# Value projections of two attentions moved behind the attentions' first scores

## The reference

```python
# first block, per layer (4 heads of 64 columns)
logits = q @ k.T * scale + f_q[:, None] - f_k[None, :]      # f: running sum of log forget gates
probs  = softmax(where(key_pos <= q_pos, logits, -inf))
out    = probs @ v                                          # v = h @ w_in[:, value columns]
# second block: for each of 3 groups of 4 heads (windows of 128, 512, 2048; dilations 1, 4, 16)
s = q_block @ k_block.T * scale + band_mask
p = softmax(s);  o = p @ v_block;  lse = log(sum(exp(s)))
out = sum over groups of softmax(lse over groups) * o
```

## Time and profile before

| | us |
|---|---|
| time, median of 3 runs (4006.53 to 4017.21) | 4011.14 |
| time of the profiled execution | 4007.0 |
| span in its trace | 4005.2 |
| PE busy | 3704.3 (92%) |
| DVE busy | 1721.3 (43%) |
| ACT busy | 1155.8 (29%) |
| POOL busy | 712.6 (18%) |

### The profile page before, as it was taken

One profiled execution on the slowest core, in us unless ns is written; L12 is line 12 of the kernel. 1 busy time (PEld: TensorE's weight loads), 2 busy tenths in 40 slices (PEclk: granted clock), 3 DMA queues, 4 the chain that ended last, 5 costly groups with the idle time before them and its releaser, 6 DMA issues. The chain is left out here.

```text
span 4005.2 us, 67440 instructions
## 1 busy us (share of the span) xinstructions
PE 3704.3 (92%) x29462; PEld 2800.3 (70%) x29462; DVE 1721.3 (43%) x3002; ACT 1155.8 (29%) x2208; POOL 712.6 (18%) x248
## 2 busy tenths in 40 slices
PE   6899998998999989899879999998899999999998
PEld 5564666886646668778757777776687568787876
DVE  6644545456445454621674544544003253223233
ACT  1427233114272331301544444443101121001011
POOL 2110003221100032122021111110221012322321
PEclk9999899999999999999989999999899999999999
DMA  4131201221302012312110000000222211111112
GB/s 155 40 95 38 66 12 61 78 74 43 95 19 84 12 57 81 126 34 72 61 36 19 25 25 28 26 24 23 72 63 86 91 42 43 53 42 53 42 49 109
DMA packets 190182, 225.67 MB, mean 56 GB/s; under 512 B 20991, under 2 KB 168001, under 8 KB 187081
## 3 DMA queue, kind: packets, MB, share of 16 engines
q1 hardware_dynamic: 189896, 221.47, 16.8%
HBM read 188.89 MB, written 32.56 MB: 55 GB/s over the span
## 5 line engine op out<-in xcount | busy, mean ns | idle before, releaser
L193 POOL CAST weights_high<-weights_value 128x2048 fp32r<-128x2048 f32 x34 | 67.0, 1970 | 1289.3 <-DMA weights_value<-in_w_in_dram 691.5
L208 PE MATMUL banks<-h_high,weights_high 128*128 128x512 f32 x608 | 241.2, 397 | 8.1 <-PEq L820 5.1
L208 PE MATMUL banks<-h_high,weights_low 128*128 128x512 f32 x608 | 238.9, 393 | 0.0
L208 PE MATMUL banks<-ffn_in_high,ffn_weights_high 128*128 128x512 f32 x512 | 203.9, 398 | 8.4 <-PEq L75 8.1
L208 PE MATMUL banks<-ffn_in_low,ffn_weights_high 128*128 128x512 f32 x512 | 203.6, 398 | 0.0
L208 PE MATMUL banks<-ffn_in_high,ffn_weights_low 128*128 128x512 f32 x512 | 203.4, 397 | 0.0
L208 PE MATMUL banks<-ffn_weights_high,hidden_high 128*128 128x512 f32 x512 | 199.2, 389 | 0.0
L208 PE MATMUL banks<-ffn_weights_low,hidden_high 128*128 128x512 f32 x512 | 199.2, 389 | 0.0
L208 PE MATMUL banks<-ffn_weights_high,hidden_low 128*128 128x512 f32 x512 | 199.2, 389 | 0.0
L4244 ACT ACTIVATE hidden_value<-banks 128x512 f32<-128x512 f32 x64 | 38.3, 598 | 555.7 <-PE banks L208 555.6
L208 PE MATMUL banks<-h_high_again,pair_weights_high 128*128 128x512 f32 x384 | 180.3, 469 | 7.1 <-PEq L2293 7.1
(11 more groups left out here) (479 smaller groups left out, 9153.5 us busy)
## 6 DMA issues: line engine op xcount, KB each, us to landing
ffn_weights_value<-in_w_ff_dram SPq DMA_DIRECT2D x32, 1024.0 KB, 5.4
weights_value<-in_w_in_dram SPq DMA_DIRECT2D x24, 1024.0 KB, 5.2
attention_scratch<-in_ada_w_dram SPq DMA_DIRECT2D x12, 1024.0 KB, 5.3
pair_weights_value<-in_w_in_dram SPq DMA_DIRECT2D x24, 512.0 KB, 4.0
ndow_weights_value<-in_w_in_dram SPq DMA_DIRECT2D x10, 1024.0 KB, 5.2
weights_value<-in_w_out_dram SPq DMA_DIRECT2D x8, 1024.0 KB, 5.2
gates_value<-in_w_in_dram SPq DMA_DIRECT2D x16, 512.0 KB, 4.8
first_mixed<-in_ada_w_dram SPq DMA_DIRECT2D x6, 1024.0 KB, 5.2
```

Source lines behind the costliest of these rows:

```text
L193: nc.gpsimd.tensor_copy(high, value).then_inc(rounded, 1)
L208: mm = nc.tensor.matmul(out, x, y, start=(first and i == 0 and j == 0), stop=(last and i == n - 1 and j == 2))
```

## The change

Four value groups (tiles 4 to 7) leave each of the three projection stages: the two edges lose their last four groups, and the window projection loses the last 4 of its 24 (`LATE_VALUES`). They are handed as `late` to the attention that follows. There PE runs them right behind scores(0), into four half banks of banks 6 and 7 (`late_place`), and ACT copies them out right behind the exponents of unit 0. PE waits for these copies before the first product with values. In the first edge the transpositions of the memory input now stand ahead of the two last key groups instead of ahead of the value groups.

```diff
+def late_place(k, i):
+    return k.psum[:, 6 + i // 2, i % 2 * 256:(i % 2 + 1) * 256]
...
 # pair_attention, PE
             def do_sum(u):
                 p = units[u][0]
                 pe.wait_ge(moved, before[u + 1])
+                if u == 0 and late:
+                    pe.wait_ge(late_moved, len(late))
...
                 if it < N:
                     do_scores(it)
+                if it == 0:
+                    for i, (pairs, dst) in enumerate(late):
+                        gemm(nc, late_place(k, i), pairs).then_inc(late_done, 1)
                 if 1 <= it <= N:
                     do_turn(it - 1)
...
 # pair_attention, ACT
                     exponent(it, 0)
                     exponent(it, 1)
+                if it == 0:
+                    for i, (pairs, dst) in enumerate(late):
+                        act.wait_ge(late_done, i // 2 * 2 + 2)
+                        nc.scalar.copy(dst, late_place(k, i)).then_inc(late_moved, 1)
...
 # boundary
-            fox += [("value", t) for t in range(4 * half, 4 * half + 4)]
+            if half == 0:
+                fox += [("value", t) for t in range(4)]
...
-                for n in range(9, 18):
-                    if mem and n == 14:
+                for n in range(9, len(fox)):
+                    if mem and n == 12:
                         do_mem()
                     do_fox(n)
...
 # first_layer
+                   late=[(over_columns(b, C_FV, t, 0, 256), values[:, t, :]) for t in range(4, NT)])
...
 # window_attention, PE (ACT as above)
+                if it == 0:
+                    for i, (pairs, dst) in enumerate(late):
+                        gemm(nc, late_place(k, i), pairs).then_inc(late_done, 1)
                 if 1 <= it <= N:
                     do_turn(it - 1)
+                if it == 2:
+                    pe.wait_ge(late_moved, len(late))
...
 # windows: PE and ACT
-            for n in range(WINDOW_GROUPS * NT):
+            for n in range(WINDOW_GROUPS * NT - LATE_VALUES):
                 values(n)
```

More of the change, by code:

```diff
@@ L774 @@
 MEM_UNITS = tuple(tuple((t, 2) for t in range(4 * i, 4 * i + 4)) for i in range(2))
+def late_place(k, i):
+    return k.psum[:, 6 + i // 2, i % 2 * 256:(i % 2 + 1) * 256]
 def pair_attention(k, name, bufs, q, key, value, out, pair_units, diagonal=None, bias=None, bias_here=(),
-                   prefetch=(), w=None, splits=(), turned_part=None):
+                   prefetch=(), w=None, splits=(), turned_part=None, late=()):
     nc = k.nc
     st = Stage(k, name)
-    names = ("scores_done", "masked", "max_ready", "exp_done", "scaled", "turned", "act_moved", "summed", "out_moved")
-    (scores_done, masked, max_ready, exp_done, scaled, turned, moved, summed, out_moved) = (st.sem(n) for n in names)
+    names = ("scores_done", "masked", "max_ready", "exp_done", "scaled", "turned", "act_moved", "summed", "out_moved",
+             "late_values_done", "late_values_moved")
+    (scores_done, masked, max_ready, exp_done, scaled, turned, moved, summed, out_moved,
+     late_done, late_moved) = (st.sem(n) for n in names)
     weights, turned_buf = bufs
@@ L1721, in _ @@
                 forget()
-                for n in range(10, 18):
+                for n in range(10, len(fox)):
                     if not on_dve[n]:
@@ L1764, in first_layer @@
     pair_attention(k, "fox" + tag, (weight_bufs, turned_bufs), half_of(qt), half_keys(kt), own, pair_tile(0), CAUSAL_UNITS,
-                   diagonal=k.causal_add, bias=mixed[:, 2:6, :], bias_here=b.forget_here, splits=(C_SQ, C_SK), w=W)
+                   diagonal=k.causal_add, bias=mixed[:, 2:6, :], bias_here=b.forget_here, splits=(C_SQ, C_SK), w=W,
+                   late=[(over_columns(b, C_FV, t, 0, 256), values[:, t, :]) for t in range(4, NT)])
     def condition(n):
@@ L2251, in window_rows, with window_attention @@
     return [(4 * run + i, i, (4 * run + i,)) for i in range(4)]
-def window_attention(k, qk, vt, weights, turned_buf, parts, masks, oat, clear, w_in, early):
+def window_attention(k, qk, vt, weights, turned_buf, parts, masks, oat, clear, w_in, early, late):
     nc = k.nc
@@ L2265, in window_attention @@
     names = ("scores_done", "max_ready", "exp_done", "scaled", "turned", "act_moved", "summed", "out_moved", "log_ready",
-             "lse_ready", "lse_spread", "lse_moved", "top_ready", "shares_ready", "shares_summed", "share_log_ready", "inverted")
+             "lse_ready", "lse_spread", "lse_moved", "top_ready", "shares_ready", "shares_summed", "share_log_ready", "inverted",
+             "late_values_done", "late_values_moved")
     (scores_done, max_ready, exp_done, scaled, turned, moved, summed, out_moved, log_ready,
-     lse_ready, spread, lse_moved, top_ready, shares_ready, shares_summed, share_log, inverted) = (st.sem(n) for n in names)
+     lse_ready, spread, lse_moved, top_ready, shares_ready, shares_summed, share_log, inverted,
+     late_done, late_moved) = (st.sem(n) for n in names)
     units = [(p, g, run) for p in range(2) for g in range(3) for run in range(2)]
@@ L2568 @@
 VALUE_ORDER = (1, 2, 0)
+LATE_VALUES = 4
 def window_weights(k, a):
@@ L2829, in windows @@
     parts = [k.x[:, i, :] for i in range(8)] + [more[:, i, :] for i in range(2)]
-    window_attention(k, qk, vt, weights, turned, parts, masks, oat, [*k.x_away, here, sin_in, cos_in, trig_step, h_away], w_in, k.early)
+    late = [([((high[:, j, t * P:(t + 1) * P], k.h_low[:, j, t * P:(t + 1) * P]), W.parts(W_LOW + WINDOW_GROUPS, j, 0, 256)) for j in range(KT)],
+             vt[:, VALUE_ORDER[-1], t, :]) for t in range(NT - LATE_VALUES, NT)]
+    window_attention(k, qk, vt, weights, turned, parts, masks, oat, [*k.x_away, here, sin_in, cos_in, trig_step, h_away], w_in, k.early, late)
 J_ORDER = (1, 0, 2)
```

## The result

| | before | after |
|---|---|---|
| median of the runs | 4009.01 us (4 runs) | 3981.40 us (3980.23 to 3987.76, 4 runs) |
| span of the profiled execution | 4005.2 us | 3980.1 us |
| PE busy | 3704.3 us, 92% | 3700.0 us, 93% |

The ratio of the runs is 0.9931, with a 95% interval of 0.9916 to 0.9947. Run once more beside the last experiments (`e11`), the same kernel gave 0.9939 (0.9924 to 0.9953). The forecast was 3981.

A forecast was written before the change was run, and what follows sets the result against it. PE, busy 92% of the span, bounds the kernel unless it idles; value groups move into its idle time. Terms saved 29.8 us: 4007.0 to 3977.2 for the profiled execution, plus 4.1 for the median, 3981 us; range 3973 to 3992.

The forecast's parts named there:

- `fox_0` up to scores(3): First forgetting attention: unit 1 is 0.9 us late, faster scores(2) give time back; 0.4 us ahead, ends -0.1 and 0.9.
- `fox_1` up to scores(3): Second forgetting attention: same as the first, but late groups take 10.9 us; 0.8 us ahead, ends 0.3 and 1.3.
- local attention up to scores(2): Scores(1) done 14.9 us after the start, where DVE began minima at 10.74; 4.15 us behind.
- The projections: Both edges and the window projection end sooner by nearly the moved groups' full price: 10.8, 10.6 and 11.35 us.
- The first cover: PE idles behind scores(0) until unit 0's exponents end: 4.92 us in `fox_0`, 5.13 us in the local attention.
- The second cover: Forgetting attention: DVE still scales unit 0 beside POOL's split, so scores(1) may come 13.6 us after block start.
- The clock: Filled gaps keep full clock: scores(1) take 1.57 us (forgetting) and 1.9 (local); scores(2) in `fox_0` 1.99 to some 3.0.
- the forget rows were issued ahead of these weights on the same queue and are there as well: Edge 0: `C_SK` lands near 115.6, needed near 118; the forget rows, issued earlier, have arrived too.
- case 2: One edge or the window projection gives nothing, held by returning values, the `C_SK` load or a barrier; 3990 us, chance 0.1.
- case 4: Slower: the late groups behind scores(0) run at half clock, matmul distance above 0.12 us; 4020 us, chance 0.02.
- DVE's scaling slide with the late groups: In both `fox` blocks scaling slides instead of hiding the late groups, 10 us each; 4001 us, chance 0.05.
- The full case: Both clock terms end well, ACT's or DVE's small additions unseen, runs' median equal to the profile; 3976 us, chance 0.2.

The follow-up runs named there:

- e11: The changed kernel itself run once more, nothing altered, against the kernel before on the same chip; 3985.12 against 4008.46 us, ratio 0.9939.
- e3: Kernel before, with the twelve late value groups added behind the first scores and the projections left whole, so those values are made twice; 4011.25 us, ratio 1.0003.
- e4: Kernel before, with late groups only in the local attention, two instead of four; 4002.42 us, ratio 0.9978.
- e8: Kernel before, with two late groups in each forgetting attention and none in the local one; 3999.74 against 4011.47 us, ratio 0.9976.
- e5: Kernel before, with POOL's split of weights in the forgetting attention held back until unit 0 is scaled; 4012.03 us, ratio 1.0006.
- e2: Changed kernel with late groups only in the two forgetting attentions; window projection and local attention as in the kernel before; 3991.97 us, ratio 0.9951.
- e7: Changed kernel, with SP loading the next query weights after two of the four forget rows instead of after all; 3986.52 us, ratio 0.9948.
- e9: Changed kernel plus useless transpositions behind turn(0), 8 in each forgetting attention and 12 in the local one; 3979.60 us, ratio 0.9925.
- e10: Changed kernel with the useless transpositions of e9 and the next query weights loaded ahead of the last two forget rows; 3976.18 us, ratio 0.9918.

## Why the prediction was right

The time was 3981.4 for 3981 forecast. The mechanism was right; that the two numbers agree to 0.4 us is luck. The forecast saved 29.8 us and started from the profiled execution, with 4.1 us added because the median before stood that much above it. One more run brought the median before to 4009.01, 2.1 us lower, and the saving was 27.6 us, 2.2 less than forecast: the two errors cancelled. Without the addition the forecast for the profiled execution was 3977.2, and it took 3981.85. The terms came out so, each from the distance of two rows in the profiles before and after:

| term | forecast | measured |
|---|---|---|
| edge 0, from the scan of the forget sums to `fox_0` | 10.8 | 10.70 |
| edge 1, the same | 10.6 | 11.04 |
| window projection, first value copy to the attention | 11.35 | 11.36 |
| `fox_0` up to scores(3) | 0.4 ahead | 0.2 behind |
| `fox_1` up to scores(3) | 0.8 ahead | 1.3 behind |
| local attention up to scores(2) | 4.15 behind | 4.56 behind |
| sum | 29.8 | 27.1 |

**The projections.** These three terms were right to 0.1, 0.4 and 0.01 us, and so was the reading that PE's products were the last thing each of these blocks waited for. The memory transpositions cost about what they did before.

**The first cover.** That PE stood idle behind the first scores and that a late group there costs nothing until the exponents are done: shown by e3 (34 us of work for at most 4.4 us) and by the head of e4.

**The second cover.** That DVE, held by POOL's split, would not need scores(1) before 13.6 us: shown by e8 (mask at 13.7 although the scores were there) and by e5. It is why four groups are worth more than two in the forgetting attentions and not in the local one.

**The clock.** Scores(1) took 1.57 and 2.00 us at 1.00, forecast 1.57 and 1.9. For scores(2) I took the middle between holding and falling. In the two profiles of the changed kernel it fell in three of four forgetting attentions: scores(2) took 2.79, 3.58, 3.58 and once 1.99 us, 3.0 on average and 2.8 with those of e2 and e7, where the middle was 2.5. So this term was too kind by 0.3 to 0.5 us. The full clock in all four attentions of e9 and e10 shows that filling part of the idle time holds it. The length of the last idle stretch alone does not decide it: in e5, where scores(1) had run at half clock, scores(2) took 2.91 us behind 1.76 us idle in `fox_0` and 1.99 us behind 2.13 us in `fox_1`. What else decides it is open.

**What failed.** The step "the forget rows were issued ahead of these weights on the same queue and are there as well" looked only at `C_SK`. The weights `C_SQ`, which POOL needs first, were 1.24 us late in `fox_1` (0.75 us in the second profile). About 0.65 us of this reached the chain (the mask at 15.06 us against 14.41 in e3) and is in the 2.1 us by which `fox_1` missed; 1.1 us more is the clock of scores(2), 3.58 us instead of the 2.5 forecast. The late groups also took 11.15 to 11.6 us from the end of scores(0) to scores(1), 0.2 to 0.3 more than in the projections.

The sum of the terms is 27.1, and the two profiled spans differ by 25.1. The other 2.0 us lie at places that the change doesn't touch; two of these places were found, and both are stretches of half clock. In the windows, PE ran the same matmuls of the first edge at 0.51 in the profile after and at 1.00 in that before:

```profile
58.60:62.00 3.40, 3.40 (x9) 0.51 0.18 77
```

and in the profile before, this place and the one named below:

```profile
58.60:62.00 3.40, 3.40 (x16) 1.00 0.18 77
291.20:298.00 6.80, 5.71 (x11) 0.50 0.00 0
```

The first put `fox_0` 1.6 us later, while the profile before had its half-clock stretch at 291.2 to 298.0, and that after had none at that place. That the runs of one kernel spread by 8 us fits this, but was not shown to come from it.

**The signs.** Scores(1) without the wait, at 1.57 us, came as written, and DVE's first mask of unit 1 at 14.8 us for 14.5; DVE's minima in the local attention began 15.3 us after its start for 14.9. The blocks began later than written: `fox_0` at 113.22 for 111.6, `fox_1` at 909.53 for 908, the local attention at 1893.01 for 1888. By the wording of the prediction this pointed to case 2, but the table excludes that case, since every projection gave its full length. The 1.6 us at `fox_0` are the half clock in the edge; of the 5 us at the local attention, 2.3 are the terms ahead of it in the table, and 2.4 are the net delay at places outside them. The sign was badly chosen, because a start also carries everything that happened before it. The late matmuls followed each other every 0.119 us in `fox_0` (96 of them, first start to last 11.29 us), inside the 0.12 of case 4 by little.

**The rivals.** The half clock for the late groups (slower) did not happen: they ran at 1.00. Its turning point of 85% does not follow from its own terms, which give 30 / (34 + 5), 77%; nothing rested on it. A stage end that does not follow did not happen either, nor did DVE's scaling slide with the late groups (4.97 us beside them, 4.87 before). The full case, 3976, was not reached by this kernel.

## What to carry to other kernels

Work that is needed late can be put behind the first step of a softmax chain for the price of what exceeds the idle time, but only that: two groups were worth as much as four where one wait was all the cover, so measure the cover by the engine that needs PE's next result, not by PE's idle time alone. When a block gets shorter, go through every load that the next block's first instructions use, in the order of the queue, not only the last one. A gap that is filled also gives back the clock of what follows; here that was 1.36 us behind a gap of 4.92 us and 1.8 us behind one of 5.13 us.

## What was not expected of the hardware

The scores of units 2 and 3 in the local attention, whose queries and keys are read with a stride of four, take 3.13 us at both granted clocks. The kernel after, windows of unit 2 and of unit 3:

```profile
1913.80:1916.90 3.10, 3.10 (x17) 0.50 0.00 0
1922.73:1925.80 3.07, 3.07 (x19) 1.00 0.00 0
```

and of e9, unit 2 again:

```profile
1909.90:1913.00 3.10, 3.01 (x16) 1.00 0.00 0
```

All three took 3.13 us in the timeline, at 0.50 and at 1.00, for 12 blocks of 128 columns, where the contiguous scores of unit 1, 16 such blocks, took 3.78 us at half and 2.00 at full clock. Something other than the array's clock bounds them. The stride is what sets them apart in the code, but no run changed it alone, so what it is stays open.

The stall beside POOL's split ends with POOL's instructions: in e5 the two slow scalings end at 139.01 and 144.06, just behind POOL's ends at 138.92 and 143.51. Moving the split moved most of the loss to the next unit (3.9 us won, 3.3 us given back).
